# Eight modulation units move from TensorE to VectorE, beside a feed-forward layer

## The reference, cut to what matters

```python
cond = jax.nn.silu(c)
for i in range(DEPTH_2):
    mod = (cond @ ada_w[i] + ada_b[i])[:, None, :]
    shift1, scale1, gate1, shift2, scale2, gate2 = jnp.split(mod, 6, axis=-1)
    h = rmsnorm(x, norm1_g[i]) * (1.0 + scale1) + shift1
    y = diff_attention(...) if i % N_MIXERS == 0 else axial_gqa(...)
    x = x + gate1 * y
    h = rmsnorm(x, norm2_g[i]) * (1.0 + scale2) + shift2
    x = x + gate2 * swiglu(h, f_w_in[i], f_w_out[i])
return rmsnorm(x, final_g)
```

## Time and profile before

| | before |
|---|---|
| median of 3 runs | 1378.43 us (1378.06 to 1382.33) |
| the profiled execution, its own time | 1377.22 us |
| its span in the trace | 1375.4 us |
| PE busy (matmuls) | 1153.6 us, 84% |
| PE busy (weight loads) | 917.0 us, 67% |
| DVE busy | 611.5 us, 44% |
| ACT busy | 540.8 us, 39% |
| memory read | 394.97 MB, 288 GB/s over the span |
| a 2 MB load of `ring<-in_wpk`, issue to landing | 8.1 us median |

### The profile page before, as it was taken

How to read it: one execution, slowest core, us unless ns; L and a number is a source line. 1 busy time by engine, 2 the same in 40 slices (tenths; PEclk the granted TensorE clock), 3 DMA queues, 4 the chain that set the end, 5 groups by cost and what they waited for, 6 DMA issues and landing times.

```text
span 1375.4 us, 22370 instructions
## 1 busy us (share of the span) xinstructions
PE 1153.6 (84%) x9627; PEld 917.0 (67%) x9627; DVE 611.5 (44%) x1363; ACT 540.8 (39%) x1203; POOL 0.2 (0%) x4
## 2 busy tenths in 40 slices
PE   6989998857475666657589989999999989999997
PEld 4867678534243443424257757999998758899997
DVE  4564664201110110101165765665555855655554
ACT  4554553211101111101155665555554654655553
POOL 0000000000000000000000000000000000000000
PEclk9999998989788889978899999999999999999999
DMA  9895847899999999999978655555546655655520
GB/s 390 345 356 223 355 186 294 341 427 427 428 426 426 424 427 427 426 426 428 426 299 307 235 194 198 231 184 184 185 153 230 228 215 184 245 184 184 184 93 31
DMA packets 29569, 397.53 MB, mean 289 GB/s; under 512 B 3480, under 2 KB 4888, under 8 KB 5400
## 3 DMA queue, kind: packets, MB, share of 16 engines
q1 hardware_dynamic: 29032, 395.72, 72.1%
q10 hardware_dynamic: 432, 0.30, 0.1%
HBM read 394.97 MB, written 1.05 MB: 288 GB/s over the span
## 4 chain that ended last, share of the span: by engine, by line
PE 61%; DMA 20%; DVE 10%; ACT 7%; issue 2%; SPq 0%; ACTq 0%; DVEq 0%
PE ps L141 61%; DMA mem<-in_w 13%; DMA ring<-in_w 5%; DVE mem L141 5%; DVE memr L141 3%; ACT mem L141 3%; ACT memr L141 3%; DMA ring<-in_wpk 1%; DVE small L141 1%; DMA posi<-in_pos 1%; ACT L141 0%; ACT rowb L141 0%; DVE x L141 0%; SPq L141 0%; DVE mcol L141 0%
## 5 line engine op out<-in xcount | busy, mean ns | idle before, releaser
L141 PE MATMUL ps<-memr 128*128 128x256 f32 (+1 forms) x4680 | 670.6, 303 | 17.9 <-DVE memr L141 17.9
L141 PEld LDWEIGHTS ps<-memr 128*128 128x128 f32 x4680 | 612.4, 193 | 62.5 <-DVE memr L141 27.8
L141 DVE TENSOR_TENSOR memr<-ring,memr 128x512 fp32r<-128x512 f32 x440 | 297.7, 690 | 247.0 <-ACT memr L141 243.6
L141 PE MATMUL ps<-mem 128*32 128x256 f32 (+5 forms) x2360 | 299.1, 421 | 86.8 <-DMA ring<-in_w 34.9
L141 ACT ACTIVATE memr<-ring 128x512 fp32r<-128x512 f32 x440 | 268.2, 627 | 221.6 <-PE ps L141 214.6
L141 PEld LDWEIGHTS ps<-mem 128*32 128x32 f32 (+3 forms) x2360 | 185.9, 150 | 158.6 <-issue 106.7
L141 ACT ACTIVATE mem<-ps 128x256 f32<-128x256 f32 (+5 forms) x307 | 121.3, 407 | 417.4 <-PE ps L141 415.4
L141 PE MATMUL ps<-ring,mem 128*32 128x256 f32 x1408 | 150.4, 428 | 40.5 <-DMA mem<-in_w 35.7
L141 DVE TENSOR_TENSOR mem<-mem,ps 128x256 f32<-128x256 f32 (+1 forms) x76 | 31.7, 418 | 270.3 <-ACT mem L141 270.3
L141 PEld LDWEIGHTS ps<-ring,mem 128*32 128x32 f32 x1408 | 72.8, 122 | 78.9 <-issue 53.3
L141 DVE COPY mem<-ps 32x256 f32<-32x256 f32 (+2 forms) x81 | 38.2, 471 | 118.7 <-PE ps L141 117.7
(11 more groups left out here) (91 smaller groups left out, 379.7 us busy)
## 6 DMA issues: line engine op xcount, KB each, us to landing
ring<-in_wpk SPq DMA_DIRECT2D x89, 2048.0 KB, 8.1
mem<-in_w SPq DMA_DIRECT2D x52, 2048.0 KB, 34.4
ring<-in_w SPq DMA_DIRECT2D x44, 2048.0 KB, 36.5
mem<-in_wpk SPq DMA_DIRECT2D x1, 2048.0 KB, 10.4
ring<-in_wpk SPq DMA_DIRECT2D x2, 1024.0 KB, 5.3
x<-in_x SPq DMA_DIRECT2D x2, 512.0 KB, 5.7
out_dram<-mem SPq DMA_DIRECT2D x4, 256.0 KB, 2.2
cst<-in_cst SPq DMA_DIRECT2D x1, 944.0 KB
```

Source lines behind the costliest of these rows:

```text
L141: ins = o[1](*o[2], **o[3])
```

## The change

Eight of the modulation units, (1,10), (1,11), (2,2), (2,3), (2,6), (2,7), (2,8) and (2,9), are taken out of the attention stretches of layers 1 and 2 and out of their places in the list. In the list they now stand in the feed-forward of layer 1, one behind the first unit and then one for every two. There a generator `ada_sums` in `side` computes them on DVE: with the condition as a scalar per partition, DVE multiplies the first 512 columns (`TENSOR_SCALAR`) and adds the other seven (`SCALAR_TENSOR_TENSOR`), one instruction for two slabs of the feed-forward, 16 slabs for a unit. Then four products with a matrix of ones (128 x 32) on PE sum over the partitions, and DVE adds the bias. The slot of such a unit is held for those 16 slabs. ACT's copies to `rowb` and the transposes of these units go. A `drain()` behind the feed-forward finishes the last unit.

```diff
--- before.py
+++ after.py
@@ -273,14 +273,18 @@
                 units.append(t[name][e])
         moe_last = len(units)
         mixed((U_AQKV, 8), ada(1, 4), (U_AQKV + 2, 8), ada(1, 5), (U_AQKV + 4, 8), ada(1, 6), ada(1, 7),
-              (U_AQKV + 1, 8), ada(1, 8), (U_AQKV + 3, 8), ada(2, 2), (U_AQKV + 5, 8), ada(2, 3),
-              (U_AWO, 8), ada(1, 9), ada(1, 10), (U_AWO + 1, 8), ada(1, 11), ada(2, 0), ada(2, 1))
+              (U_AQKV + 1, 8), ada(1, 8), (U_AQKV + 3, 8), (U_AQKV + 5, 8), (U_AWO, 8), ada(1, 9), (U_AWO + 1, 8),
+              ada(2, 0), ada(2, 1))
+        beside = [(1, 10), (1, 11), (2, 2), (2, 3), (2, 6), (2, 7), (2, 8), (2, 9)]
         for i in range(2):
-            mixed(*[(U_FIN + 11 * i + n, 8) for n in range(11)],
-                  *[(U_FOUT + 6 * i + n, 8 if n < 5 else 4) for n in range(6)])
+            seq = [(U_FIN + 11 * i + n, 8) for n in range(11)] + [(U_FOUT + 6 * i + n, 8 if n < 5 else 4) for n in range(6)]
             if i == 0:
-                mixed(ada(2, 4), ada(2, 5), (U_BQKV, 8), (U_BQKV + 2, 8), (U_BQKV + 1, 8), (U_BWO, 8), ada(2, 6), ada(2, 7),
-                      ada(2, 8), (U_BWO + 1, 8), ada(2, 9), ada(2, 10), ada(2, 11))
+                for n, (l, u) in enumerate(beside):
+                    seq.insert(3 * n + 1, ada(l, u))
+            mixed(*seq)
+            if i == 0:
+                mixed(ada(2, 4), ada(2, 5), (U_BQKV, 8), (U_BQKV + 2, 8), (U_BQKV + 1, 8), (U_BWO, 8), (U_BWO + 1, 8),
+                      ada(2, 10), ada(2, 11))
 
         state = {"load": 0, "use": 0, "recs": {}, "slot": {}, "last": {}}
 
@@ -417,6 +421,35 @@
                 rc = A(sc.activation, rowb[:, z, :], ps[:, :], ACT.Copy, after=[r] + rowb_free[z])
                 PB.give(b, [rc])
                 ada_open.append((i, n, z, rc))
+
+        def ada_sums(todo):
+
+            for i, n in todo:
+                w, ld = unit("cols")
+                m = in_use.pop()
+                z = ada_n[0] % 2
+                ada_n[0] += 1
+                acc, r = rowb[:, z, :], None
+                for k in range(8):
+                    c = csb[:, 0 if i == 0 else 1, k, 0:1]
+                    if k == 0:
+                        r = V(vt.tensor_scalar, acc, w[:, k, :], c, None, ALU.mult, after=[ld, cs_r[1]] + rowb_free[z])
+                    else:
+                        r = V(vt.scalar_tensor_tensor, out=acc, in0=w[:, k, :], scalar=c, in1=acc, op0=ALU.mult,
+                              op1=ALU.add, after=[r])
+                    yield
+                    yield
+                load_unit(state["slot"][m], [r])
+                b, ps, fr = PB.take()
+                for c in range(4):
+                    r2 = mm(ps[:, 32 * c:32 * c + 32], acc[:, 128 * c:128 * c + 128], ones[:, 0:32], True, True,
+                            after=fr + [r, ld_c1])
+                rowb_free[z] = [r2]
+                rv = V(vt.tensor_tensor, mcol[:, i, 4 * n:4 * n + 4],
+                       ps[:, 0:128].rearrange("p (c r) -> p c r", c=4)[:, :, 0],
+                       cols[:, C_ADA + 48 * i + 4 * n:C_ADA + 48 * i + 4 * n + 4], ALU.add, after=[r2])
+                PB.give(b, [rv])
+                ada_rec[(i, n)] = rv
 
         def ada_unit(i, n):
 
@@ -1765,15 +1798,12 @@
                 ada_unit(1, 8)
                 side.append(paced(at_, [1] * 8))
                 qk_unit(qT, 2, 0.125, qt_r, 1, free_a)
-                ada_unit(2, 2)
                 qk_unit(kT, 0, 1.0, kt_r, 1, qt_r[0])
-                ada_unit(2, 3)
                 side.append(paced(at_, [4, 0, 0, 0]))
                 h2_last = v_unit(1)
                 drain()
                 next(at_)
                 ada_unit(1, 9)
-                ada_unit(1, 10)
                 side.append(paced(at_, [0] * 9))
             else:
                 qr2, kr2 = [[], []], []
@@ -1841,10 +1871,7 @@
                 queue(turn(qst1[0], qr2[0], qT[:, 0:4, :], free_a, qt_r[0]))
                 queue(*k_steps, turn(kvb, kr2, kT, free_a, kt_r[0], 0, 2))
                 _, h2_last = project(h2, h2_r, q_ev(1))
-                ada_mm(2, 6)
                 drain()
-                ada_copy()
-                ada_close(True)
                 last_q = chain(*later)
                 for s_ in range(12):
                     if s_ == 8:
@@ -1854,8 +1881,6 @@
                             pass
                     next(at_)
                     next(last_q, None)
-                    if s_ in (1, 4):
-                        ada_unit(2, 7 if s_ == 1 else 8)
                 side.append(paced(at_, [0] * 8))
             h2_free = [h2_last]
             wo1, _ = fold_out(c2_, c_r, (0, 1, 2, 3), i, 0, x_r)
@@ -1863,7 +1888,6 @@
             for _ in at_:
                 pass
             ada_close(True)
-            ada_unit(*((1, 11) if i == 1 else (2, 9)))
             nm = Norm()
             x_r, c_last = fold_out(c2_, c_r, (4, 5, 6, 7), i, 0, wo1, nm)
             ada_close(True)
@@ -1877,6 +1901,8 @@
             g_fr = [[c_last] for _ in range(4)]
             for n in range(11):
                 bk, ff_last = project_T(h2, h2_r, 128, 256)
+                if i == 1 and n == 0:
+                    side.append(ada_sums(beside))
                 for m in range(2):
                     f = 2 * n + m
                     z = f % 4
@@ -1908,6 +1934,7 @@
             nm = Norm()
             x_r, _ = fold_out(act2, f_r, tuple(range(22)), i, 1, x_r, nm)
             if i == 1:
+                drain()
                 ada_mm(2, 4)
             rB_r = nm.close()
             if i == 1:
```

## The result

| | before | after |
|---|---|---|
| median of 15 runs each, on the same chip | 1379.81 us (1377.08 to 1383.59) | 1387.05 us (1381.34 to 1392.61) |
| ratio | | 1.0044, interval 1.0031 to 1.0057 |
| profiled execution, its own time | 1377.22 us | 1390.32 us |
| its span | 1375.4 us | 1388.5 us |
| PE, PEld, DVE, ACT busy | 1153.6, 917.0, 611.5, 540.8 us | 1154.4, 925.6, 649.5, 536.1 us |

The changed kernel is slower, by 6 us by the ratio and 7 by the medians. The forecast was 1381.2, so the time lies 5.9 us above it: inside the range of 1373 to 1390, but just above the 1376 to 1386 that the forecast's own mechanism was given.

A forecast was written before the change was run, and what follows sets the result against it. PE was taken as full in the feed-forward, with room on DVE and transfers, and as holding most of layer 1's attention chain. -15.9 + 7.0 + 0.3 + 8.9 + 2.5 = +2.8 gave 1380.0, forecast 1381.2 us, range 1373 to 1390.

The forecast's parts named there:

- the forecast's own mechanism: Whole kernel: removals offset by added sums, a later load and a lowered clock; 1381.2 us, range 1376 to 1386, chance 0.48.
- the removals: Attentions of layers 1 and 2: taking eight units off PE saves 15.9 us, between 12 and 19.7.
- the sums: Layer 1's feed-forward: four added PE products per unit cost 1.0 us; seven units 7.0, bounds 5.6 and 9.1.
- DVE: Layer 1's feed-forward: multiply-adds, about 0.7 us each in a queue, just fit; cost 0.3 us, bounds 0 and 4.
- the fourth rival: Attentions: the softmax chain sets the pace, so removals give 12 with a stall of 10; 1386 to 1388 us, chance 0.10.
- The ring and the end of the feed-forward: Layer 1's feed-forward end: load four slabs later, 5.8 us; with queued multiply-adds and sums 8.9, bounds 7.5 and 10.
- the clock: From the norm on, behind PE's wait of about 8 us: some 5 us at half rate, +2.5, bounds 0 and 5.
- The third rival: After the long wait, the clock stays low through the norm into the projections: 5 us more, 1386, chance 0.13.
- the second rival: Feed-forward: VectorE becomes the bound from 0.9 us per multiply-add; at 1.1 us each, 9 us more, 1390, chance 0.15.
- all four removed units stood inside the long PE pieces: Layer 1's attention: (2,2), (2,3), (1,10), (1,11) each save 1.79 + 0.40; 8.8 us, bounds 7 and 9.
- In layer 2 7.1 was said: Layer 2's attention: removing (2,6) to (2,9) saves 3.5, 0.6, 0.8 and 2.2, together 7.1 us, bounds 5 and 10.6.
- the likeliest case: Whole kernel: no change that a measurement tells, its limit being 0.3% or 4.1 us; chance 0.44.

The follow-up runs named there:

- e1_seven: Seven units: the changed kernel with (2,9) put back on PE in layer 2; 1376.81 us, ratio 0.9963 to the kernel before.
- e12_one: The changed kernel with only the eighth unit at one multiply-add per slab, its sums a slab later; 1384.93 us, ratio 1.004 to the kernel before.
- e7_warm: The changed kernel with 60 unused dummy products on PE ahead of the norm's first product; 1385.8 us, ratio 1.0038 to the kernel before.
- e8_double: Seven units on DVE, with a second, zero-scalar multiply-add behind each one; 1399.49 us, ratio 1.0128 to the kernel before.
- e6_four: The changed kernel with (2,2), (2,3), (2,7), (2,8) back on PE; 1374.19 us, ratio 0.996. Its mark: a PE timeline row 63.91 us after unit (1,8).
- e3_hold: The changed kernel with staging held for the last three slabs, so copies awaiting the late load follow the update of `x`; 1377.35 us, ratio 0.9982.
- e5_tail2: The changed kernel with its last two units at one multiply-add per slab and their sums a slab later; 1380.97 us, ratio 0.9999.
- e9_three: Three units on DVE: e6_four with (2,9) also put back on PE; 1377.33 us, ratio 0.998 to the kernel before.

## Why the prediction was right, and where it was not

The time lies in the stated range, and the mechanism at the end of the feed-forward was the one forecast. That the forecast missed by only 5.9 us has a part of luck in it: against the two traces, the removals were put 6.6 us too high, and the sums and DVE 1.6 too high the other way. Of the 5.9, 1.4 come from the kernel before itself, whose fifteen runs have their median at 1379.81 and the three shown at 1378.43. The measured 1387.05 is what the fourth rival said, 1386 to 1388, with a chance of 0.10: 12 us of removals and a stall of 10.

**The ring and the end of the feed-forward: right.** Predicted 8.9, and 2.5 for the clock, together 11.4. Measured 11.8 to 12.0: against seven units 11.8; against before, 12.58 + 4.90 less the seven sums of 5.67 gives 11.8 as well, and PE's last product to the projections went from 6.94 to 18.92, 12.0. Single terms: the load came 6.2 us later relative to PE (10.1 to 3.85; 5.8 predicted), alone it costs 5.1 (e12_one); two multiply-adds stood before the update as said, and the wait was 8.32 where 1.25 + 5.8 + 1.4 = 8.45 was said. The rest was put at 0.7 for the wait of the last sums, 1.0 for the sums and 2.5 for the clock, 4.2, and the stretch grew by 4.90. e7_warm divides it: with the clock at 1.00 the sums do wait 0.75, and wait and sums together make 1.83 (7.52 - 5.69); the other 3.1 are the clock's, within the bound of 5. The third rival, a low clock until the projections, did not come: the level was back before 1080.66, where the six wide products take 1.66 us, as in the other kernels. The Trainium skill, "TensorE: Matmul & The Clock Gate", section "What's actually happening", has the slow level as the default and activity as what releases it; the trace agrees with its busy window at 0.50.

**The sums: a little less than said.** 0.81 for each, 1.0 taken, bounds 0.8 and 1.3 right: 5.7 instead of 7.0.

**DVE: right in this kernel, its limit too low.** 0.746 us for a multiply-add and 0.66 in a queue, against 0.745 and 0.7; no new wait in the middle, 0 instead of 0.3; 15.9 to 16.4 busy of 20 where about 17 was said. But the second rival's limit, PE waiting in every unit from 0.9 us per multiply-add on, did not show. With about 1.4 us the prediction's formula gives 4 x 0.7 - 0.7 = 2.1 for each feed-forward unit, and e8_double's PE waited 2.7 for the copies in the whole piece. What cost there were the late sums and the clock behind them.

**The removals: the terms that were mis-sized.** 15.9 was said; the two stretches gave 3.83 and 5.49, 9.3. (The upper end of the range for them, 19.7, adds up to 19.5 from its own terms, which changes nothing.)

In layer 1 the step was "all four removed units stood inside the long PE pieces: 4 x (1.79 + 0.40) = 8.8 us", bounds 7 to 9. A piece of the chain on PE says that PE was not waiting, not by how much the softmax's results were there before PE wanted them. Without the two units PE waited for them 0.79, 0.79 and 1.38 us: (2,2) and (2,3) gave 1.6 instead of 4.4. This was the fourth rival's mechanism, with a chance of 0.10, in the very layer in which I held it excluded. For (1,10) and (1,11) 4.4 was nearly right: from the mark of e6_four on to the feed-forward it takes 58.99 before and 55.07 in e6_four, 3.9 less. In after it took 56.76, and the clock fell at just that place (0.83 in the window from 800 to 820, 1.00 before): 1.7 given back.

The other traces warn against taking these figures as fixed. The same program from that mark to the feed-forward took 56.7 to 56.8 in four of the traces without the two units and 55.6 in the other five, and in these five the feed-forward's first 192 products took 23.3 us instead of 24.8. With the two units on PE, as in e6_four, it took 55.1 or 57.2 (two traces each). Counted from unit (1,8) to the end of those 192 products, before's one trace needs 147.67, after 143.87 and the five 141.2: the four units gave 3.8 to 6.5 us in layer 1, below the 7 to 9 said in either case.

In layer 2 7.1 was said. From the wait of 1.87 at 1117.83 (1100.75 before, both 37.17 us behind the start of the projections) to the eight transposes at 1134.37 (1121.53 before) it is 16.54 instead of 20.78, 4.24 less, where (2,6) to (2,8) had been put at 4.1. From there to the feed-forward it is only 1.25 less, where the transposes and (2,9) had been put at 3.0. In seven units (2,9) is on PE and the stretch is the same to 0.01, but in the other traces with eight units on VectorE it is 111.0 to 112.2, and 112.4 in all three with (2,9) alone back on PE: (2,9) gave 0 to 1.3, where 2.2 was said. A part of what is missing is the wait of 0.71 shown above. Against before's program, 117.87 and 116.21 in its two traces, the four units of layer 2 gave 3.8 to 6.8. The clock was at 0.76 in after's window from 1120 to 1140; before has 0.95 from 1103 to 1123, which lies as far behind its projections. So another part is the clock's; how much is open.

**The sum with the measured terms,** those of the two traces in the table: -3.8 - 5.5 + 5.7 + 11.8 = +8.2, against +2.8. The 5.4 between them are 6.6 of removals too many, 1.6 too much for sums and DVE, and 0.4 too little for the end. The medians say 7.2, and their ratio 6.1. So the likeliest case, no change that can be told, was missed: the runs say slower, by 0.44%, which had a chance of 0.40. The end was worked out well, and the removals were taken nearly whole.

**Open:** how much of each attention's loss is clock and how much softmax; no experiment held the clock up there. The kernel before has two traces of layer 2's part and one of layer 1's, too few for its own scatter. The times of versions with two to seven units lie between 0.996 and 0.998 with intervals of about 0.003, so their order is not shown. Each of them beats both kernels (e3_hold's interval reaches 1.0002); e6_four is the lowest.

## What to carry to other kernels

Before work is added to a queue of loads, count which release issues the load that is late already: here one unit more in the list turned a gain of 0.4% (e1_seven) into a loss of 0.4%. What a late load costs is set by what stands behind the copies that wait for it: ordering the last update ahead of them saved most of it, with the load as late as ever. And a long piece of one engine in the chain says nothing about what comes when it is made shorter: look how long before their use the other engines' results were there.

Read a lost microsecond's releaser before naming the bound: in e8_double DVE was nearly full and PE lost time, but PE waited for one late result and then ran at a lowered clock.

## What the runs showed of the hardware that I had not expected

PE's granted clock falls at short waits as well, and not at the same place in each run of one program. After a wait of 3.06 us two products took 1.22 instead of 0.70 (e5_tail2); after waits of 1.42 they did not. In e8_double the clock fell to 0.57 behind a wait of 1.18 (window 930 to 934), and stayed at 1.00 behind one of 1.16 (904 to 920). In the attention of layer 1 the window from 800 to 820 had 0.83 in after and 1.00 in before and e6_four; in e3_hold, whose program there is that of after, it had 1.00, and the next window 0.91. One program for one stretch differed by 1.7 to 2.2 us between traces, for instance layer 1's attention 118.98 in e6_four, 121.09 in e9_three, whose window from 800 to 820 had 0.91. Windows of after:

```profile
800.00:820.00 20.00, 17.36 (x90) 11.00 (x91) 11.28 (x25) 12.85 (x38) 0.00 (x0) 0.83 0.20 68
...
1120.00:1140.00 20.00, 14.96 (x55) 10.88 (x54) 13.48 (x31) 12.33 (x51) 0.00 (x0) 0.76 0.00 1
```

The runs' spread of some 8 us goes with the clock: in seven units, the two shortest runs, 1370.8 and 1371.7, had a mean clock of 0.944 and 0.945, and those at 0.938 took 1378.8 and 1378.9. I take it that removing PE work from a stretch with waits lets the clock fall more often and so take back what was saved, but that is not shown: of the nine traces without (2,2) and (2,3) four have the dip to 0.83 and five do not.
